# Fifteen taps of the long convolution's last two chunks computed by TensorE from diagonal blocks

## The reference, cut to what matters

```python
def even_mixer(h, w_in, conv_w, conv_b, ln_g, ln_b, pool_w, pool_b, pool_scale, w_out):
    p = jnp.einsum("btd,dn->btn", h, w_in)
    a_val, a_glu, a_gate, b_val, b_gate = jnp.split(p, [...], axis=-1)
    u = a_val * jax.nn.sigmoid(a_glu)
    u = causal_depthwise_conv(u, conv_w, conv_b)      # 31 taps, each channel with weights of its own
    u = jax.nn.silu(layernorm(u, ln_g, ln_b))
    ya = u * jax.nn.silu(a_gate)
    d = multiscale_pool_diff(b_val)...                # then a small matrix per group ("pool")
    yb = (d + pool_b) * pool_scale * jax.nn.silu(b_gate)
    return jnp.einsum("btn,nd->btd", jnp.concatenate([ya, yb], -1), w_out)
```

## Time and profile before

| | us |
|---|---|
| median of 3 executions | 1165.42 |
| the profiled execution | 1167.06 |
| its span | 1165.3 |
| TensorE matmul busy | 1078.4 (93%) |
| VectorE busy | 758.8 (65%) |
| GpSimd busy | 600.3 (52%) |
| ScalarE busy | 597.2 (51%) |

### The profile page before, as it was taken

The page is one execution under the profiler, slowest core; times in us unless marked ns, Lnnn a source line. Parts: engine busy times, 40 slices in busy tenths (PEclk is TensorE's granted clock), DMA queues, the critical chain, the costliest instruction groups (busy, mean ns, idle before and its releaser), DMA issues. The chain is left out here.

```text
span 1165.3 us, 21433 instructions
## 1 busy us (share of the span) xinstructions
PE 1078.4 (93%) x8189; PEld 1006.8 (86%) x8189; DVE 758.8 (65%) x1506; ACT 597.2 (51%) x1188; POOL 600.3 (52%) x453
## 2 busy tenths in 40 slices
PE   8899999999999989999999999989997879866886
PEld 8699978988889979999999999989887779655886
DVE  8859586666553245864855533369999795675964
ACT  4345667666664467644455543443334354656442
POOL 3546344445544477555344443386775654542661
PEclk9989999999999989999999999999999888888998
DMA  8224333333234423245455555544443324333342
GB/s 304 92 91 145 112 107 105 113 128 109 91 110 145 145 76 107 91 156 185 162 181 185 182 182 179 168 161 165 162 150 124 125 91 143 112 102 108 120 142 73
DMA packets 43445, 158.08 MB, mean 136 GB/s; under 512 B 4944, under 2 KB 4944, under 8 KB 43088
## 3 DMA queue, kind: packets, MB, share of 16 engines
q1 hardware_dynamic: 43200, 156.69, 39.8%
q10 hardware_dynamic: 144, 0.03, 0.0%
HBM read 155.65 MB, written 1.05 MB: 134 GB/s over the span
## 5 line engine op out<-in xcount | busy, mean ns | idle before, releaser
L1731 PE MATMUL p_proj<-arena_r,ring_hi 128*128 128x256 f32 x2208 | 661.5, 300 | 28.8 <-POOL ring_lo L548 11.1
L1732 PE MATMUL p_proj<-arena_r,ring_hi 128*128 128x256 f32 x2208 | 630.9, 286 | 0.0
L1733 PE MATMUL p_proj<-arena_r,ring_lo 128*128 128x256 f32 x2208 | 630.3, 285 | 0.0
L548 POOL TENSOR_TENSOR ring_lo<-ring,ring_hi 128x1024 fp32r<-128x1024 f32 x182 | 438.3, 2410 | 349.4 <-ACT ring_hi L877 348.5
L1731 PEld LDWEIGHTS p_proj<-arena_r,ring_hi 128*128 128x128 f32 x2208 | 429.1, 194 | 48.4 <-issue 28.3
L1732 PEld LDWEIGHTS p_proj<-arena_r,ring_hi 128*128 128x128 f32 x2208 | 430.0, 195 | 7.9 <-issue 6.0
L1733 PEld LDWEIGHTS p_proj<-arena_r,ring_lo 128*128 128x128 f32 x2208 | 429.5, 195 | 0.0
L877 ACT ACTIVATE ring_hi<-ring 128x1024 fp32r<-128x1024 f32 x276 | 290.4, 1053 | 118.8 <-PE p_proj L1733 117.8
L548 DVE TENSOR_TENSOR ring_lo<-ring,ring_hi 128x1024 fp32r<-128x1024 f32 x94 | 119.6, 1272 | 67.4 <-ACT ring_hi L877 65.9
L653 POOL TENSOR_TENSOR sbuf_s<-sbuf_s,srow 128x256 f32<-128x256 f32 (+1 forms) x48 | 41.8, 870 | 83.1 <-DVE srow L1301 58.5
L1720 PE MATMUL p_proj<-arena,ring 128*128 128x256 f32 x208 | 59.3, 436 | 24.9 <-issue 12.0
(11 more groups left out here) (274 smaller groups left out, 1243.0 us busy)
## 6 DMA issues: line engine op xcount, KB each, us to landing
ring<-w_stream SPq DMA_DIRECT2D x289, 512.0 KB, 3.3
arena<-w_tok SPq DMA_DIRECT2D x1, 1632.0 KB, 13.4
arena<-x_t SPq DMA_DIRECT2D x4, 256.0 KB, 4.9
arena<-w_cmp SPq DMA_DIRECT2D x1, 1024.0 KB, 15.3
out_t<-arena SPq DMA_DIRECT2D x4, 256.0 KB, 2.4
par<-cols SPq DMA_DIRECT2D x1, 323.0 KB, 3.0
row<-rows ACTq DMA_DIRECT2D x1, 32.0 KB, 3.2
```

Source lines behind the costliest of these rows:

```text
L548: return eng.tensor_tensor(ring_lo[:, u % RING, :, :].rearrange("p k n -> p (k n)"), ring[:, u % RING, :, :].rearrange("p k n -> p (k n)") ...
L1731: pe.matmul(slot(s)[:, 0:S], w_hi, hi, start=(c == 0), stop=False)
L1732: pe.matmul(slot(s)[:, 0:S], w_hi, lo, start=False, stop=False)
L1733: mm = pe.matmul(slot(s)[:, 0:S], w_lo, hi, start=False, stop=(c == n - 1))
```

## The change: 15 taps of chunks 6 and 7 by TensorE

A new job "cvt" of 32 blocks (four units, 2 MB) is put into the stream and into TensorE's order behind b_gate 7 and ahead of pool 0. For each of chunks 6 and 7 it has 15 diagonal blocks (one for each of the taps 0 to 14) and one diagonal block with the bias, which is multiplied with ones. They are plain fp32 and accumulate in `p_pv`, where VectorE then adds taps 15 to 30. Of the econv steps of pair 3, 24 to 27 are dropped, and 28 starts at tap 15. Its inputs in `ub` are made by an own step ("ubp",) behind b_gate 0. Step 28 waits for the whole cvt job, and cvt waits for ubp. The cvt job takes no `p_proj` bank, and its units are not split.

```diff
+PE_TAPS = 15
-          ("a_gate", 8, 8), ("pool", 8, 2), ...
+          ("a_gate", 8, 8), ("cvt", 1, 32), ("pool", 8, 2), ...
-PLAIN = {"b_val", "pool", "rg_ig"}
+PLAIN = {"b_val", "pool", "cvt", "rg_ig"}
...
+    pieces = [("econv", n) for n in range(32) if not 24 <= n < 28]
-    for job in first + jobs["b_gate"] + pool[0:4] + a_gate[0:4] + pool[4:8] + a_gate[4:8]:
+    for job in first + jobs["b_gate"] + jobs["cvt"] + pool[0:4] + a_gate[0:4] + pool[4:8] + a_gate[4:8]:
         out.append(job)
+        if job == jobs["b_gate"][0]:
+            out.append(("ubp",))
...
-        if columns >= 40 and conv < min(32, (columns - 12) // 10):
+        if columns >= 40 and conv < min(28, (columns - 12) // 10):
...
+                elif k == "ubp":
+                    was_read(dve, ("job", "val_glu", 15))
+                    for cc in (6, 7):
+                        dve.scalar_tensor_tensor(out=ub[:, cc, 30:30 + S], in0=A(TA + cc), scalar=1.0, in1=A(VA + cc),
+                                                 op0=ALU.add, op1=ALU.mult).then_inc(sem("ub_ready"), 1); note(sem("ub_ready"))
...
+                    if c == 6 and eighth == 4:
+                        dve.wait_ge(filled["proj"], filled_at["job", "cvt", 0])
-                    for tap in range(4 * eighth + (eighth == 0), min(4 * eighth + 4, CONV_K)):
+                    for tap in range(PE_TAPS if c == 6 and eighth == 4 else 4 * eighth + (eighth == 0), min(4 * eighth + 4, CONV_K)):
...
+                    if name == "cvt":
+                        was_read(pe, ("uB", 15), "D")
+                        pe.wait_ge(sem("ub_ready"), 2)
+                        for c in range(n):
+                            b, cc, tap = b0 + c, 6 + c // 16, c % 16
+                            if c == 0 or b % 8 == 0:
+                                pe.wait_ge(w_in[b // 8 % RING], 16 * (b // 8 // RING + 1))
+                            mm = pe.matmul(bank["pv"][0][:, S * (cc - 6):S * (cc - 6) + S], ring[:, b // 8 % RING, b % 8, :],
+                                           ub[:, cc, tap:tap + S] if tap < PE_TAPS else ones[:, 0:1].to_broadcast([P, S]),
+                                           start=(tap == 0), stop=(tap == PE_TAPS))
+                            if b % 8 == 7 or c == n - 1:
+                                mm.then_inc(filled["proj"], 1)
+                        continue
```

More of the change, by code:

```diff
@@ L50 @@
           ("ff1", 32, 8), ("ff2", 8, 32), ("val_glu", 16, 8), ("b_val", 8, 8), ("b_gate", 8, 8),
-          ("a_gate", 8, 8), ("pool", 8, 2), ("even_yb", 8, 8), ("even_ya", 8, 8), ("xr", 12, 8), ("gate", 12, 8),
+          ("a_gate", 8, 8), ("cvt", 1, 32), ("pool", 8, 2), ("even_yb", 8, 8), ("even_ya", 8, 8), ("xr", 12, 8), ("gate", 12, 8),
           ("rg_ig", 24, 1), ("odd_out", 8, 12)]
@@ L233, in schedule @@
         columns += {"pool": 2, "b_val": 10}.get(job[1], 8)
-        if columns >= 40 and conv < min(32, (columns - 12) // 10):
+        if columns >= 40 and conv < min(28, (columns - 12) // 10):
             for _ in range(2 if job[1] in ("b_val", "a_gate") else 1):
-                if conv < min(32, (columns - 12) // 10):
-                    out.append(("econv", conv))
+                if conv < min(28, (columns - 12) // 10):
+                    out.append(pieces[conv])
                     conv += 1
@@ L242, in schedule @@
             out += [("split", "yb", 2 * (job[2] // 4 * 2 + job[2] % 4 // 2) + job[2] % 2)]
-    out += [("econv", n) for n in range(conv, 32)]
+    out += pieces[conv:]
     out += [("ln",)] + even_yb[0:3] + [("lnv",)] + even_yb[3:5]
@@ L314, in psum_tenants @@
         k = s[0]
-        if k == "job":
+        if k == "job" and s[1] != "cvt":
             add("proj", s, "D" if s[1] in ON_VECTOR else "AD" if s[1] in TWICE or s[1] == "rg_ig" and s[2] % 2 else "A")
@@ L934, in _ @@
                     act.activation(A(FFS + j % 4), A(FFR + j % 4), ACT.Square).then_inc(sem("ffs_ready"), 1); note(sem("ffs_ready"))
-                elif k == "job" and s[1] not in ON_VECTOR:
+                elif k == "job" and s[1] not in ON_VECTOR and s[1] != "cvt":
                     _, name, j = s
@@ L1756 @@
     odd = a["w_in_odd_2"][0]
+    taps = a["conv_a_w_2"][0].reshape(31, 8, 128)
+    cvt = np.zeros((2, 16, 128, 128), np.float32)
+    for c in range(2):
+        for t in range(16):
+            np.fill_diagonal(cvt[c, t], taps[t, 6 + c] if t < PE_TAPS else a["conv_a_b_2"].reshape(8, 128)[6 + c])
     weights = {
+        "cvt": cvt.reshape(1, 32, 128, 128),
         "iq": tiles(iq), "ik": tiles(np.concatenate([ik] * 4, axis=1)), "dk": tiles(np.concatenate([dk, dk], axis=1)),
```

## The result

| | before | after |
|---|---|---|
| median of 7 executions, us | 1165.42 (1160.27 to 1169.09) | 1171.74 (1168.31 to 1174.90) |
| profiled execution, us | 1167.06 | 1174.90 |
| its span, us | 1165.3 | 1173.2 |
| TensorE busy, us | 1078.4 | 1091.3 |
| VectorE busy, us | 758.8 | 744.1 |

The ratio is 1.0056, 95% interval 1.0031 to 1.0081: the change costs 6.5 us (3.6 to 9.4). Forecast were 5.4 us and 1170.8.

A forecast was written before the change was run, and what follows sets the result against it. VectorE was taken to set the stretch from b_gate 7 to ln, with 9.67 us of TensorE idle. 7.85 (stretch) + 0.5 (ubp) - 2.93 (ln's clock) = +5.4 us on 1165.42 gave 1170.8, range 1166.7 to 1175.0.

The forecast's parts named there:

- The sum: TensorE's stretch from b_gate 7's end to ln: 49.65 us against 41.80 before, 7.85 us more.
- From pool 4 to ln: Pool 4 and 5 take 1.89 us, pool 6 to a_gate 7 13.5; no wait for a_gate 3's read, ln at once.
- Cvt's term: TensorE's 32 plain fp32 blocks behind b_gate 7, priced as four times b_val's 3.62 us: 14.48 us.
- ubp: Pair 3's two input operations, moved behind b_gate 0, delay TensorE by 0.5 us; 1.3 if GpSimd holds them up.
- Ln's clock: With no idle spell ahead of it, ln takes 3.72 us in place of 6.65: 2.9 us less.
- its signs of being wrong: Cvt records near 0.12, TensorE idle while cvt waits, ln slow again, or the traces' difference arising behind ln.
- The net: Whole kernel: 7.85 + 0.5 - 2.93 = +5.4 us, giving a median of 1170.8 us.
- A: Rival: step 4's low clock stays away and ubp is free; 1168.7 us, or 1167.7 with less idle; chance 0.20.
- step 4: Pool 2 and 3 and a_gate 0 to 3 as before: 14.89 us, including 1.6 us of low clock.
- B: Rival: dearer ubp, slowed pool multiplies and a second low-clock stretch; up to 1174.7 us; chance 0.14.
- C: Rival: cvt fits TensorE's idle time at 0.12 us a record; 1164.0 us, or 1162.4; chance 0.04.
- D: Rival: the 10.74 us low-clock stretch behind lnv comes out at full clock, up to 4 us less; 1166.8 us; chance 0.07.

The follow-up runs named there:

- e6: Kernel before, no taps on TensorE, pair 3's steps spread one each behind b_gate 4, 5, 7 and a_gate 0 to 6; -2.6 us by the ratio.
- e8: Against the kernel before: 3 taps and bias on TensorE, cvt between b_gate 4 and 5, rest of pair 3 spread; -1.6 us by the ratio.
- e10: Same kernel as e8, measured again against the kernel before; -2.7 us (-4.4 to -0.8) by the ratio.
- e1: Changed kernel, but VectorE reads b_gate 7 before step 28 waits for cvt; +2.4 us (0.7 to 4.2) against the kernel before by the ratio.
- e2: Changed kernel without the cvt job, taps 0 to 14 of chunks 6 and 7 left out; -8.2 us against the kernel before by the ratio.
- e3: Changed kernel with cvt kept, but VectorE makes all 31 taps itself; +11.3 us (9.0 to 13.8) against the kernel before by the ratio.
- e7: The change's 15 taps, but cvt between b_gate 4 and 5 and pair 3's rest spread; 0.0 us against the kernel before by the ratio.

## Why the prediction was right

- **The sum.** 49.65 us were forecast for the stretch, 48.60 measured. Idle ahead of pool 2: 3.0 against 3.01. Pool 2 to a_gate 3: 14.89 against 14.91, low clock included. From pool 4 to ln: 15.4 against 14.96, with no idle spell. Cvt: 14.48 against 13.83. VectorE's stall: 13 against 13.59; its last tap near 905 (counted from 1.8 us earlier) against 906.75.
- **Where the sum was too dear.** Cvt's term was mis-sized from its own rows. The 3.62 us of a b_val job run to the end of its last record, which is 0.38 long, while the next record starts 0.216 us behind it; four times 3.62 counts that overhang four times. From start to start the rows give less: b_val at 786.28 and the next at 792.61 are 6.33 us apart, and 24 split matmuls (2.88) lie between, so 16 records are 3.45 us, 0.216 each, exactly what cvt took. The same overhang (0.16, behind pool 5) and ln's start 0.2 us ahead of a_gate 7's tanh make most of the 0.4 between 15.4 and 14.96.

```profile
792.61 2.75 PE L1720 MATMUL p_proj<-arena,ring 128*128 128x256 f32 x12
```

- **ubp.** Charged 0.5 us, cost nothing: its two operations, from 855.00 on, took 0.76 us for both, so the second (0.42) had begun by 855.34, just ahead of GpSimd, which then took 2.60 us in place of 2.41:

```profile
855.43 2.60 POOL L552 TENSOR_TENSOR ring_lo<-ring,ring_hi 128x1024 fp32r<-128x1024 f32 x1 [1.48 <-ACT ring_hi L881]
```

  That operations with two SBUF inputs wait for GpSimd stands, as e6 shows (6.46 against 1.81 us). That ubp escaped by a tenth of a microsecond is my reading of the two starts; no run moves them apart. The prediction's 3.2 us for ubp under that rule is a slip too: from 853.18 to GpSimd's end at 856.02 are 2.8, 0.9 us of cost in place of 1.3.
- **Ln's clock.** 2.9 us forecast, 3.0 measured. The step that failed stands right behind it: "Everything behind ln hangs on it in the same order, so it only moves." Lnv took 5.38 us in place of 3.69, 1.7 us given back, so that a part of the difference did arise behind ln, which the prediction had among its signs of being wrong. e8 and e10 show that this clock differs between executions of one kernel, so no sum over the order could have given it.
- **The net.** By the trace +3.8 up to ln and +5.5 up to lnv, where +5.4 was forecast; two errors of about 1.6 us (stretch and ubp too dear, lnv not seen) met. So the mechanism was right and the closeness of 5.5 to 5.4 is luck. The ratios say 6.5 (3.6 to 9.4) and 5.1 (2.3 to 7.8); both intervals hold the +3.8 as well, and they can't tell which share lnv's clock has over many executions.
- **The rivals.** A (the low clock of step 4 stays away) did not happen in either profile: pool 2 to a_gate 0 took 6.41 us at 0.73. B was not needed. C fell with cvt's 0.216 a record (its "ln" at full clock is lnv's row; ln ran at 0.56). D did not happen: the stretch that it names was at the low clock again (964.75 to 975.49 at 0.53), and lnv went the other way.
- **The cause.** e1, e2, e3 and e7 part it, by the traces up to ln: the relief is worth 8 to 10 us (4.8 to 8.2 by the ratios), cvt costs 13.4, and about 4.7 of the cost is its place and what is queued behind its wait.

## What to carry to other kernels

Moving work to the engine that is busier overall pays only up to its idle time in that very stretch: 3.5 us of it left VectorE the bound, 6.9 fitted into 9.7, 13.8 did not. Put the wait for the moved work behind the reads that free the other engine's banks, and start the work early enough for the waiting engine to have something else to do. Check after such an order change where the next read in the same loop has come to stand. And take the price of a matmul from the distance between starts: a merged row's time counts the overhang of its last record, 0.16 us here, once for every row.

## What the runs showed of the hardware

- A spell of low clock can come or go for one and the same program: lnv's 16 records, behind 1.88 and 1.90 us of idle TensorE, took 5.38 us in e8 and 3.69 in e10, one kernel; over the thirteen profiles it was 5.38 nine times and 3.69 four times, once of them in the kernel before. A profile's 1.7 us there are not to be put down to a change. Behind 1.85 us of idle at about 783 us it was the same: full clock in the kernel before, 0.97 over 750 to 800 us in the other twelve.
- A plain fp32 block with a broadcast column as moving operand, or one that starts at a tap's offset, costs what a plain one does: 0.43 us for two records (32 blocks of cvt in 13.83 us, a b_val job's eight in 3.45).
- VectorE's operations with both inputs in SBUF vary from 0.42 to 2.67 us each beside GpSimd's ring_lo (pool's multiplies: up to 2.51 in the changed kernel, 2.67 in e6); the taps, with one input in PSUM, keep to 0.40.
